# Convolution's ends reordered, norm and projection in one block; the last block's sixteen row copies issued by three engines

## Chip, core and metric

One core of a Trainium2 chip runs the kernel. Its engines are TensorE (PE in the profile, its weight loads PEld), VectorE (DVE), ScalarE (ACT), GpSimd (POOL) and SyncE (SP), which only issues transfers. ACT and POOL can issue transfers too. The metric is the device time of one execution in microseconds (us), as the median of several.

## What is computed

One step of a two-layer decoder trunk for 512 prompt tokens and 8 x 4 sample tokens (544 in all), 1024 channels, float32. Layer 0 mixes by sliding-window attention, layer 1 by a convolution module; each is followed by a mixture of 32 experts. The change is in the convolution module:

```python
def conv_module(h, hist, w_pw1, b_pw1, w_dw, b_dw, ln_g, ln_b, w_pw2, b_pw2):
    a = jnp.einsum('btd,de->bte', h, w_pw1) + b_pw1
    u = a[..., :D_CONV] * jax.nn.sigmoid(a[..., D_CONV:])
    ext = jnp.concatenate([hist.astype(u.dtype), u], axis=1)
    c = lax.conv_general_dilated(ext, w_dw[:, None, :].astype(ext.dtype), ...) + b_dw   # 31 taps, each channel by itself
    c = jax.nn.silu(layer_norm(c, ln_g, ln_b))
    y = jnp.einsum('btc,cd->btd', c, w_pw2) + b_pw2
    return y, ext[:, -(CONV_WIDTH - 1):]
```

Its input h is rmsnorm(x); x = x + y follows, then the experts on rmsnorm(x).

## The kernel before

Activations lie with channels on the 128 partitions: eight slices (KT = 8) of 128 channels by 544 tokens, a row of 544 being two halves of 272 (TH). A product in nearly full precision is made of float32r halves: a weight or operand is split into a high part (ACT, `high` and `x_high`) and a low part (DVE, or GpSimd for some, `low` and `x_low`), and TensorE adds high x high, high x low and low x high. So 128 output columns are 8 slices x 3 products x 2 halves of the tokens = 48 matmuls. The class `Columns` holds this: two weight buffers s, the semaphores `ready` (split), `projected` (multiplied), `x_ready`.

Each engine has its own list of instructions, in the order in which its function writes them, and waits on semaphores; there is no planner. A `nc.Block()` ends when all engines are through; `semaphores_back()` clears semaphores between stages, with a barrier of all engines.

`conv_stage` works in eight blocks of 128 channels. TensorE's order is written out: `value_columns(0)`, `gate_columns(0)`, the sums of squares for the rms norm (`square_sums`), the turning of the tap weights (`turn_taps`), and then for k = 1 to 7 values(k), gates(k), taps(k-1), sums(k-2), and at the end sums(6), taps(7), sums(7). The 31 taps of a block are shared: twenty on TensorE, by matmuls over `u_quads`, a copy of the block's rows in four shifts, and eleven on DVE, a chain of instructions each waiting for the one before. The copy is sixteen transfers of 32 partitions from SBUF to SBUF, eight issued by SP and eight by ACT (`load_quads`). DVE's `finish(k)` adds TensorE's taps to its own; `sums(k)` is the column sum for the layer norm's mean. GpSimd adds the squares in pairs, spreads tap weights (`weigh`) and does the taps of the sample tokens (`samples`). Before block 0, DVE's `x_low` instructions, the four copies of the convolution's history and a memset stand mixed in one list, and ACT's `x_high` and `square` alternate.

`layernorm_stage` is a block of its own: DVE subtracts the mean (eight instructions), ACT squares, TensorE sums the squares with a matrix of ones (128 output columns, so that every partition gets the sum), ACT takes the root over 128 x 544. TensorE also turns rows that DVE then copies out and SP stores. After it comes `semaphores_back()`, and then `project_back_stage`: a reciprocal over 128 x 544, then slice by slice scaling (DVE), silu and `x_high` (ACT), `x_low` (DVE or GpSimd), first all of column block 0, then all of column block 1, then six more, each added to x by DVE (`add`). SP loads router weights, the later columns, and then the first three experts' weights; the expert stage follows.

## Time and profile before

| | us |
|---|---|
| median of 3 runs | 1113.31 |
| lowest, highest | 1110.83, 1115.28 |
| the profiled execution, its own time | 1110.85 |
| its span from first to last instruction | 1108.8 |
| TensorE busy, mean granted clock | 929.0 (84%), 0.921 |

The span is what the trace covers; what lies around it is 2.05 us in this execution. All times below are us from the span's start in that one execution. The convolution stage lies at 533 to 710, the layer norm at 710 to 721, the projection at 722 to 790. A busy time in one stretch is summed over an engine's instructions, and overlapping matmuls are counted once.

### The profile page before, as it was taken

What the parts mean: (1) busy time and instruction counts of PE and PEld (TensorE: products, weight loads), DVE (VectorE), ACT (ScalarE), POOL (GpSimd) and SP (SyncE); (2) the same over time, 40 slices, a digit from 0 to 9 for tenths busy, and PEclk for the clock granted to TensorE, in tenths of its full rate; (3) what the DMA queues carried; (4) which work ended last, traced back from release to release, by engine and by line L of the source; (5) the groups of instructions that cost most, each with busy time, mean ns of one, the idle gap of its engine ahead of it and who ended that gap; (6) DMA issues with size and microseconds to landing.
All of it is one profiled execution on the core that took longest, in us unless ns stands there. A gap on an engine that the chain in (4) does not pass through costs nothing. (4 is left out here: it accounts for less than half of the span.)

```text
span 1108.8 us, 18939 instructions
## 1 busy us (share of the span) xinstructions
PE 929.0 (84%) x7248; PEld 674.9 (61%) x7248; DVE 421.2 (38%) x948; ACT 286.1 (26%) x591; POOL 271.3 (24%) x423
## 2 busy tenths in 40 slices
PE   6999988967997788884679999669869988788757
PEld 5878878954554455553677877359645545454535
DVE  5167763263111111113768786573551111111115
ACT  6356561132111111111521111262312111111103
POOL 0800000014432322221234353120033432322120
PEclk8999999978999998997789999889969998898998
DMA  7521112695999999965534452325859999999925
GB/s 232 162 52 39 39 40 59 247 397 208 418 417 417 418 417 417 420 274 187 135 79 119 116 144 56 79 65 219 363 216 388 415 417 418 418 419 419 390 81 200
DMA packets 111690, 277.55 MB, mean 250 GB/s; under 512 B 35404, under 2 KB 73628, under 8 KB 86986
## 3 DMA queue, kind: packets, MB, share of 16 engines
q1 hardware_dynamic: 96054, 253.74, 60.0%
q0 software_dynamic: 11424, 17.87, 4.4%
q10 hardware_dynamic: 4132, 4.86, 1.8%
q8 instruction: 51, 0.84, 0.3%
q14 instruction: 29, 0.24, 0.1%
HBM read 266.25 MB, written 27.45 MB: 265 GB/s over the span
## 5 line engine op out<-in xcount | busy, mean ns | idle before, releaser
L1763 PE MATMUL ps<-ring,areaB 128*64 128x256 f32 x672 | 170.7, 412 | 38.3 <-issue 22.4
L1797 DVE COPY areaB<-ps 128x512 f32<-128x512 f32 x66 | 45.6, 691 | 378.3 <-PE ps L1780 378.3
L1764 PE MATMUL ps<-ring,areaB 128*64 128x256 f32 x672 | 171.1, 413 | 0.0
L1763 PEld LDWEIGHTS ps<-ring,areaB 128*64 128x64 f32 x672 | 96.2, 148 | 90.0 <-issue 30.8
L1809 POOL DMA_INDIRECT pair_rows<-areaB,idx x66 | 67.8, 1027 | 276.6 <-DVE areaB L1797 257.9
L1788 ACT ACTIVATE v_rows<-ps 128x256 f32<-128x256 f32 x66 | 25.3, 383 | 294.0 <-PE ps L1764 294.0
L1022 PE MATMUL ps<-conv_x_high,pw_halves 128*128 128x272 f32 x512 | 91.3, 298 | 9.6 <-DVE conv_x_low L1302 5.4
L1764 PEld LDWEIGHTS ps<-ring,areaB 128*64 128x64 f32 x672 | 96.1, 148 | 0.0
L1022 PEld LDWEIGHTS ps<-conv_x_high,pw_halves 128*128 128x128 f32 x512 | 76.0, 195 | 12.1 <-DVE conv_x_low L1302 5.3
L1804 POOL DMA_INDIRECT areaC<-h_rows,idx x66 | 68.6, 1039 | 55.8 <-issue 44.5
L1780 PE MATMUL ps<-ring,areaB 128*64 128x512 f32 x336 | 79.9, 593 | 1.4 <-DVE areaB L1794 1.4
L1785 ACT ACTIVATE areaB<-ps 128x512 f32<-128x512 f32 x66 | 39.4, 597 | 149.6 <-PE ps L1755 149.6
L1755 PEld LDWEIGHTS ps<-ident,areaC 128*128 128x128 f32 x264 | 28.8, 145 | 64.0 <-issue 48.7
L451 PE MATMUL ps<-mix_x_high,w_halves_A 128*128 128x272 f32 x320 | 59.7, 298 | 6.2 <-DVE w_halves_A L814 6.2
L1763 PE MATMUL ps<-areaA,areaB 128*64 128x256 f32 x192 | 48.6, 411 | 12.9 <-issue 10.5
L1763 PE MATMUL ps<-h_T,areaB 128*64 128x256 f32 x192 | 48.8, 413 | 12.3 <-issue 10.8
L1755 PE MATMUL ps<-ident,areaC 128*128 128x128 f32 x264 | 45.1, 295 | 14.2 <-DMA areaC<-h_rows,idx 14.2
L1022 PE MATMUL ps<-x_high,w_halves_C 128*128 128x272 f32 x256 | 47.3, 300 | 11.1 <-POOL x_low L1000 10.3
L1347 DVE SCALAR_TENSOR_TENSOR ps<-areaB,chan,ps 128x512 f32<-128x512 f32 x72 | 54.4, 756 | 2.6
L629 PE MATMUL ps<-o_high,w_halves_A 128*128 128x272 f32 x256 | 52.1, 297 | 3.7 <-DVE o_low L947 2.2
L1563 POOL IOTA areaS<- 128x10 f32 x2 | 0.3, 157 | 223.1 <-POOLq L113 171.6
L1022 PE MATMUL ps<-conv_x_low,pw_halves 128*128 128x272 f32 x256 | 54.3, 294 | 0.0
(348 smaller groups left out, 1806.7 us busy)
## 6 DMA issues: line engine op xcount, KB each, us to landing
ring<-in_w_gate SPq DMA_DIRECT2D x40, 1024.0 KB, 22.8
ring<-in_w_up SPq DMA_DIRECT2D x40, 1024.0 KB, 28.2
ring<-in_w_down SPq DMA_DIRECT2D x40, 1024.0 KB, 27.9
areaA<-in_w_gate SPq DMA_DIRECT2D x12, 1024.0 KB, 23.1
areaA<-in_w_up SPq DMA_DIRECT2D x12, 1024.0 KB, 28.7
wring<-in_w_down SPq DMA_DIRECT2D x12, 1024.0 KB, 28.1
h_T<-in_w_gate SPq DMA_DIRECT2D x12, 1024.0 KB, 23.6
h_T<-in_w_up SPq DMA_DIRECT2D x12, 1024.0 KB, 29.6
```

The costliest lines, as they stand in the source:

```text
L451: mm = pe.matmul(ps[:, bank + c, 0:TH], w[:, s, which, k, :], x[:, k, c * TH:(c + 1) * TH], start=(k == 0 and which == 0 and x is x_high), ...
L629: mm = pe.matmul(ps[:, 2 + n % 2 + 2 * c, 0:TH], w[:, s, which, k, :], o[:, k, c * TH:(c + 1) * TH], start=(k == 0 and which == 0 and o is ...
L1022: mm = pe.matmul(ps[:, 2 * s + c, 0:TH], self.w[:, s, w, k, :], self.x[x][:, k, c * TH:(c + 1) * TH], start=(k == 0 and w == 0 and x == 0) ...
L1347: steps.link(v.scalar_tensor_tensor(vec_acc if j < CW - 1 else c_T[:, k, 0:NP], shifted(k, j), col(k, V_DW + j), vec_acc, ALU.mult, ALU.add))
L1755: mm = pe.transpose(ps[:, odd, j * P:(j + 1) * P], rows_in[:, s, j * P:(j + 1) * P], ident[:, :])
L1763: pe.matmul(ps[0:CAP, 2 + odd, 0:F], rows, ring_gate(ws)[:, k, :], start=(k == 0), stop=(k == KT - 1))
L1764: mm = pe.matmul(ps[CAP:P, 2 + odd, 0:F], rows, ring_up(ws)[:, k, :], start=(k == 0), stop=(k == KT - 1))
L1780: mm = pe.matmul(ps[c * CAP:(c + 1) * CAP, 5 + odd, :], hid_T[:, s, k, :], ring_down(ws)[:, k, c * HALF:(c + 1) * HALF], start=(k == 0), s ...
L1785: return nc.scalar.activation(rows_T[:, s].rearrange("p j r -> p (j r)"), ps[:, odd, :], ACT.Copy)
L1797: return v.tensor_copy(rows_out[:, s, :], ps[:, 5 + odd, :])
L1804: return gp.indirect_dma_start(rows_in[:, s, :], None, h_half_rows, bass.IndirectOffsetOnAxis(idx[:, s:s + 1], 0), bounds_check=2 * T - 1, ...
L1809: return gp.indirect_dma_start(pair_half_rows, bass.IndirectOffsetOnAxis(idx[:, RING + s:RING + 1 + s], 0), rows_out[:, s, :], None, bound ...
```

## The change

- **Head of `conv_stage`.** ACT makes all eight `x_high` first, then splits the gate weights, then squares; then it splits the value weights of block 1, ahead of the root. DVE makes all eight `x_low` first, then the gate weights' low half, then copies the history, then the low half of block 1's value weights, ahead of the reciprocal; in block 0 it scales the values before the gates. SP loads block 1's weights before it waits for the history.
- **Tail of `conv_stage`.** DVE runs `finish(6)` before its own taps of block 7. Block 7's sixteen copies are issued six by SP, six by ACT, four by GpSimd, which has them ahead of its `samples(7)` and signals on a semaphore of its own; TensorE's taps wait for both. SP issues the first `w_pw2` columns here.
- **Norm and projection** are one block, `layernorm_project_stage`; `semaphores_back()` stands before it. ACT splits both first columns' high halves before the squares. The sums of squares use 64 output columns for each half of the tokens, side by side on the partitions; root and reciprocal work on 128 x 272, and two matmuls spread the result over the partitions into PSUM, where DVE's scaling reads it. DVE makes both low halves between the reciprocal and the scaling. TensorE does column blocks 0 and 1 together, slice by slice, after which the others follow as before. SP stores the turned rows before it loads the later columns.

The diff, cut (what is left out in the new function are lines that stood in the two old ones):

```diff
-            def x_lows(self, v, source, scale=None):
...
             def multiply(self, pe, s, n, first=False):
                 pe.wait_ge(self.ready[s], n + 1)
                 for k in range(KT):
                     if first:
                         pe.wait_ge(self.x_ready[k % 2], k // 2 + 1)
-                    for w, x in ((0, 0), (0, 1), (1, 0)):
-                        for c in range(2):
-                            mm = pe.matmul(ps[:, 2 * s + c, 0:TH], self.w[:, s, w, k, :], self.x[x][:, k, c * TH:(c + 1) * TH],
-                                           start=(k == 0 and w == 0 and x == 0), stop=(k == KT - 1 and w == 1))
+                    mm = self.multiply_part(pe, s, k)
                 mm.then_inc(self.projected[s], 1)
+            def multiply_part(self, pe, s, k):
+                for w, x in ((0, 0), (0, 1), (1, 0)):
+                    for c in range(2):
+                        mm = pe.matmul(ps[:, 2 * s + c, 0:TH], self.w[:, s, w, k, :], self.x[x][:, k, c * TH:(c + 1) * TH],
+                                       start=(k == 0 and w == 0 and x == 0), stop=(k == KT - 1 and w == 1))
+                return mm
...
-        def project_back_stage(name, w, w_halves, operand, norm, offset, l, rows_stored, stores):
...
+                quarter = lambda i: [(i, g) for g in range(4)]
+                def load_quads(eng, k, copies, landed=None):
                     eng.wait_ge(u_done, 2 * k + 2)
                     after(eng, taps_done, k - 1)
-                    for i in shifts:
-                        for g in range(4):
-                            eng.dma_start(u_quads[32 * i:32 * i + 32, k % 2, g, :],
-                                          u_T[32 * g:32 * g + 32, k, i:i + UQ]).then_inc(quads_landed[k % 2], 16)
+                    for i, g in copies:
+                        eng.dma_start(u_quads[32 * i:32 * i + 32, k % 2, g, :],
+                                      u_T[32 * g:32 * g + 32, k, i:i + UQ]).then_inc(landed or quads_landed[k % 2], 16)
                 @block.sync
                 def _(sp):
...
-                    sp.wait_ge(hist_ready, 1)
                     for k in range(KT):
                         for i in range(2):
                             if k + 1 < KT:
                                 sp.wait_ge(cols.ready[i], k + 1)
                                 sp.dma_start(wring[:, i], columns(w, (k + 1) * P + i * D)).then_inc(cols.landed[i], 16)
-                        load_quads(sp, k, (0, 1))
+                        if k == 0:
+                            sp.wait_ge(hist_ready, 1)
+                        load_quads(sp, k, quarter(0) + quarter(1)[0:4 if k + 1 < KT else 2])
+                    for i in range(2):
+                        sp.wait_ge(cols.ready[i], KT)
+                    first_columns(sp, "w_pw2", w_pw2[0], (0, P))
                     sp.wait_ge(stored, 16)
...
                     def taps(k):
                         pe.wait_ge(tap_weights_ready, k + 1)
-                        pe.wait_ge(quads_landed[k % 2], 16 * 16 * (k // 2 + 1))
+                        pe.wait_ge(quads_landed[k % 2], 16 * 16 * (k // 2 + 1) - (64 if k == KT - 1 else 0))
+                        if k == KT - 1:
+                            pe.wait_ge(last_quarter_landed, 64)
...
                     cols.high(act, 0, 0)
                     for k in range(KT):
                         x_high(k)
+                    cols.high(act, 1, 0)
+                    for k in range(KT):
                         square(k)
-                    cols.high(act, 1, 0)
+                    cols.high(act, 0, 1)
                     act.wait_ge(summed, 1)
                     nc.scalar.activation(half(std), sum_banks, ACT.Sqrt, scale=1.0 / D, bias=eps_col).then_inc(rooted, 1)
                     act.wait_ge(tap_cols_turned, 1)
                     nc.scalar.activation(tap_cols_flat, pe_acc[:, 0:KT * 4 * QUADS], ACT.Copy).then_inc(tap_cols_kept, 1)
                     for k in range(KT):
-                        if k + 1 < KT:
+                        if 0 < k < KT - 1:
                             cols.high(act, 0, k + 1)
                         sigmoid(k)
                         if k + 1 < KT:
                             cols.high(act, 1, k + 1)
-                        load_quads(act, k, (2, 3))
+                        load_quads(act, k, quarter(2) + (quarter(3) if k + 1 < KT else quarter(1)[2:4]))
...
                     cols.low(v, 0, 0)
-                    v.wait_ge(state_turned, 1)
                     for k in range(KT):
                         x_low(k)
-                        if 1 <= k <= 4:
-                            copy_history((k - 1) // 2, (k - 1) % 2)
-                        if k == 5:
-                            v.wait_ge(hist_copied, 4)
-                            v.memset(u_T[:, :, 0:HIST], 0.0).then_inc(hist_ready, 1)
                     cols.low(v, 1, 0)
+                    v.wait_ge(state_turned, 1)
+                    for i in range(2):
+                        for c in range(2):
+                            copy_history(i, c)
+                    v.wait_ge(hist_copied, 4)
+                    v.memset(u_T[:, :, 0:HIST], 0.0).then_inc(hist_ready, 1)
+                    cols.low(v, 0, 1)
                     v.wait_ge(rooted, 1)
                     v.reciprocal(rstd, std).then_inc(inverted, 1)
                     v.wait_ge(inverted, 1)
-                    def scale(k):
+                    def scale_gate(k):
...
+                    def scale_value(k):
...
                     for k in range(KT):
-                        if k + 1 < KT:
+                        if 0 < k < KT - 1:
                             cols.low(v, 0, k + 1)
-                        scale(k)
+                        if k == 0:
+                            scale_value(k)
+                        scale_gate(k)
+                        if k > 0:
+                            scale_value(k)
                         glu(k)
                         if k + 1 < KT:
                             cols.low(v, 1, k + 1)
+                        if k == KT - 1:
+                            finish(k - 1)
                         taps(k)
-                        if k >= 1:
+                        if 0 < k < KT - 1:
                             finish(k - 1)
                     finish(KT - 1)
...
                     for k in range(KT):
                         if k + 1 < KT:
                             weigh(k + 1)
+                        else:
+                            load_quads(gp, k, quarter(3), last_quarter_landed)
                         samples(k)
...
-        def layernorm_stage():
+        def layernorm_project_stage(l):
...
+            ln_sq = areaS[:, 2048:2048 + 2 * T].rearrange("p (b t) -> p b t", b=2)
+            rstd_rows = ln_std[:, 0:TH]
+            rstd_wide = ps[:, 4:6, 0:TH]
...
             with nc.Block() as block:
+                @block.sync
+                def _(sp):
...
+                    sp.wait_ge(u_kept, 2)
+                    sp.dma_start(conv_prompt[0, 0], tail).then_inc(u_stored, 16)
+                    for b in range(NB):
+                        sp.dma_start(conv_sample[0, b, HIST - NQ:HIST, :], fresh[NQ * b:NQ * b + NQ, :]).then_inc(u_stored, 16)
+                    with sp.Fori(1, 4) as n:
+                        for s in range(2):
+                            sp.wait_ge(cols.ready[s], n)
+                            sp.dma_start(wring[:, s], columns(w_pw2[0], (2 * n + s) * P)).then_inc(cols.landed[s], 16)
+                    for s in range(3):
+                        load_gateup(sp, l, s, s)
+                        load_down(sp, l, s, s)
+                    sp.wait_ge(u_stored, 16 * (1 + NB))
+                @block.gpsimd
+                def _(gp):
+                    for k in range(0, KT, 2):
+                        cols.x_low(gp, c_T, k)
                 @block.tensor
                 def _(pe):
...
                     for k in range(KT):
+                        pe.wait_ge(ln_squared, k + 1)
+                        for c in range(2):
+                            mm = pe.matmul(ps[64 * c:64 * c + 64, 4, 0:TH], ones[:, 0:64], ln_sq[:, k % 2, c * TH:(c + 1) * TH],
+                                           start=(k == 0), stop=(k == KT - 1))
+                        mm.then_inc(ln_summed, 1)
+                    pe.wait_ge(inverted, 1)
+                    for c in range(2):
+                        mm = pe.matmul(rstd_wide[:, c, :], ones[64 * c:64 * c + 1, :], rstd_rows[64 * c:64 * c + 1, :], start=True, stop=True)
+                    mm.then_inc(spread, 1)
...
+                    pe.wait_ge(u_kept, 2)
+                    for s in range(2):
+                        pe.wait_ge(cols.ready[s], 1)
+                    for k in range(KT):
+                        pe.wait_ge(cols.x_ready[k % 2], k // 2 + 1)
+                        for s in range(2):
+                            mm = cols.multiply_part(pe, s, k)
+                            if k == KT - 1:
+                                mm.then_inc(cols.projected[s], 1)
...
                 @block.vector
                 def _(v):
...
+                    v.wait_ge(rooted, 1)
+                    v.reciprocal(rstd_rows, rstd_rows).then_inc(inverted, 1)
+                    for s in range(2):
+                        cols.low(v, s, 0)
+                    v.wait_ge(spread, 1)
+                    v.wait_ge(centred, KT)
+                    for k in range(KT + 2):
+                        if k < KT:
+                            v.tensor_tensor(half(c_T[:, k, :]), half(c_T[:, k, :]), rstd_wide, ALU.mult).then_inc(scaled, 1)
+                        if k >= 3 and k % 2:
+                            cols.x_low(v, c_T, k - 2)
...
                 @block.scalar
                 def _(act):
+                    for s in range(2):
+                        cols.high(act, s, 0)
                     for k in range(KT):
                         act.wait_ge(centred, k + 1)
                         if k >= 2:
+                            act.wait_ge(ln_summed, k - 1)
+                        nc.scalar.activation(ln_sq[:, k % 2, :], c_T[:, k, :], ACT.Square).then_inc(ln_squared, 1)
+                    act.wait_ge(ln_summed, KT)
+                    nc.scalar.activation(rstd_rows, ps[:, 4, 0:TH], ACT.Sqrt, scale=1.0 / D, bias=eps_col).then_inc(rooted, 1)
+                    for k in range(KT):
+                        act.wait_ge(scaled, k + 1)
+                        nc.scalar.activation(c_T[:, k, :], c_T[:, k, :], ACT.Silu,
+                                             scale=chan[:, k, V_LNG:V_LNG + 1], bias=chan[:, k, V_LNB:V_LNB + 1]).then_inc(out, 1)
+                        act.wait_ge(out, k + 1)
+                        cols.x_high(c_T, k)
...
-        layernorm_stage()
         semaphores_back()
-        project_back_stage("w_pw2", w_pw2[0], w_halves_C, c_T, True, V_BPW2, 1, u_stored, 1 + NB)
+        layernorm_project_stage(1)
```

## Rows read from the trace of the kernel before

**Rows 1.** Busy us by stretch: PE, PEld, DVE, ACT, POOL, granted clock, transfers.

```profile
569.50:574.20 4.70, 4.67 (x21) 4.67 (x22) 4.36 (x7) 1.08 (x2) 3.47 (x4) 0.51 0.41 99
574.20:583.80 9.60, 9.60 (x78) 9.47 (x76) 7.25 (x9) 1.06 (x1) 3.42 (x7) 1.00 0.68 175
569.50:688.40 118.90, 118.86 (x932) 97.70 (x932) 92.20 (x122) 17.61 (x20) 49.84 (x76) 0.98 0.46 118
...
729.40:734.40 5.00, 4.76 (x18) 4.16 (x19) 5.00 (x7) 4.38 (x7) 1.49 (x2) 0.50 0.34 104
```

**Rows 2.** Instructions of three lines, head: ns min/median/max, first to last start.

```profile
L1271 ACT ACTIVATE conv_x_high<-x_T,chan x8: 731/734/738, 535.3 to 543.6; 128x544 fp32r<-128x544 f32 x8
...
L1302 DVE SCALAR_TENSOR_TENSOR conv_x_low<-x_T,chan,conv_x_high x8: 656/1054/1882, 536.7 to 547.6; 128x544 fp32r<-128x544 f32 x8
...
L1370 POOL TENSOR_TENSOR h_T<-h_T x4: 1344/1352/1599, 537.8 to 545.0; 128x544 f32<-128x544 f32 x4
```

**Rows 3.** Timeline, 556 to 571: start, us, engine, line, [idle before, releaser].

```profile
556.78 3.83 PE L1221 MATMUL ps<-h_T,ones 128*128 128x272 f32 x16
...
561.39 3.55 DVE L1322 RECIPROCAL areaS<-areaS 128x544 f32<-128x544 f32 x1 [11.84 <-ACT areaS L1287]
...
564.96 0.40 PE L1231 MATMUL ps<-ident,ring 31*32 31x5 f32 x17 [2.27 <-issue]
...
568.77 0.71 DVE L1331 TENSOR_TENSOR areaS<-ps,areaS 128x544 f32<-128x544 f32 x1
...
569.53 0.82 PE L1022 MATMUL ps<-conv_x_high,pw_halves 128*128 128x272 f32 x2 [4.18 <-DVE areaS L1331]
...
570.61 1.23 DVE L993 TENSOR_TENSOR pw_halves<-wring,pw_halves 128x1024 fp32r<-128x1024 f32 x1
```

**Rows 4.** Transfers issued from 569 to 710: KB each, median us to landing.

```profile
wring<-in_w_pw SPq DMA_DIRECT2D x13, 512.0 KB, 5.4
ring<-areaB SPq DMA_DIRECT2D x64, 66.0 KB, 2.1
```

**Rows 5.** Timeline, tail of the convolution, 688 to 710.

```profile
688.43 4.50 PE L1241 MATMUL ps<-ring,areaS 128*32 128x512 f32 x40
...
691.09 4.97 SPq L1183 DMA_DIRECT2D ring<-areaB  x8
691.09 5.32 ACTq L1183 DMA_DIRECT2D ring<-areaB  x8
...
691.95 7.09 DVE L1347 SCALAR_TENSOR_TENSOR ps<-areaB,chan,ps 128x512 f32<-128x512 f32 x9
...
697.21 0.24 POOL L1395 TENSOR_TENSOR areaA<-areaA,chan 128x32 f32<-128x32 f32 x1
...
699.85 0.69 DVE L1352 TENSOR_TENSOR areaA<-ps,areaA 128x512 f32<-128x512 f32 x1
...
702.71 5.01 PE L1241 MATMUL ps<-ring,areaS 128*32 128x512 f32 x40
...
708.55 1.19 PE L1249 MATMUL ps<-areaA,ones 128*128 128x272 f32 x4 [0.82 <-DVE areaA L1352]
```

**Rows 6.** Instructions of one line: GpSimd's indirect transfers in the expert stages.

```profile
L1809 POOL DMA_INDIRECT pair_rows<-areaB,idx x66: 981/1032/1042, 271.4 to 1073.7; - x66
```

**Rows 7.** Timeline, norm and projection, 710 to 754.

```profile
710.03 0.29 DVE L1433 COPY areaS<-areaB 128x256 f32<-128x256 f32 x1 [1.53 <-PEq L1177]
...
720.18 0.71 ACT L1457 ACTIVATE areaS<-ps,small 128x544 f32<-128x544 f32 x1
...
722.00 1.06 ACT L989 ACTIVATE w_halves_C<-wring 128x1024 fp32r<-128x1024 f32 x1 [1.10 <-PEq L113]
...
729.46 0.79 PE L1022 MATMUL ps<-x_high,w_halves_C 128*128 128x272 f32 x2 [9.35 <-POOL x_low L1000]
...
753.06 0.71 PE L1066 MATMUL ps<-areaB,ones 128*64 128x256 f32 x4
```

**Rows 8.** Instructions of one line: the projection's silu on ACT.

```profile
L1121 ACT ACTIVATE areaA<-areaA,chan x8: 825/827/841, 726.4 to 737.1; 128x544 f32<-128x544 f32 x8
```

More of the change, by code:

```diff
@@ L1001, in x_low @@
                                   ALU.subtract).then_inc(self.x_ready[k % 2], 1)
-            def x_lows(self, v, source, scale=None):
-                for k in range(KT + 2):
-                    if scale and k < KT:
-                        scale(k)
-                    if k == 1:
-                        self.low(v, 0, 0)
-                    if k >= 3 and k % 2:
-                        self.x_low(v, source, k - 2)
-                self.low(v, 1, 0)
             def multiply(self, pe, s, n, first=False):
@@ L1425, in _, with sums @@
+                    mm.then_inc(spread, 1)
+                    def sums(k, s, first, last):
                         pe.wait_ge(squared, k + 1)
                         for c in range(2):
-                            mm = pe.matmul(ps[:, 2 + c, 0:TH], ones[:, :], sq[:, k % 2, c * TH:(c + 1) * TH],
-                                           start=(k == 0), stop=(k == KT - 1))
+                            mm = pe.matmul(ps[64 * c:64 * c + 64, 6, 0:(256, T - 256)[c]], ones[:, 0:64], sq[:, s, (0, 256)[c]:(256, T)[c]],
+                                           start=first, stop=last)
@@ L1431, in _, with turn @@
+                    def turn(n):
+                        for s in range(2):
+                            pe.wait_ge(added[s], n)
+                            cols.multiply(pe, s, n)
+                            sums(2 * n + s - 2, s, isinstance(n, int) and n == 1 and s == 0, False)
+                    turn(1)
+                    with pe.Fori(2, 4) as n:
+                        turn(n)
+                    for s in range(2):
+                        sums(KT - 2 + s, s, False, s == 1)
                 @block.vector
@@ new lines, in add @@
+                    def add(n, last):
+                        for s in range(2):
+                            v.wait_ge(cols.projected[s], n + 1)
+                            xs = half(x_T[:, ds(2 * n + s, 1), :].rearrange("p k t -> p (k t)"))
+                            off = chan[:, ds(2 * n + s, 1), V_BPW2:V_BPW2 + 1].rearrange("p k n -> p (k n)")
+                            v.scalar_tensor_tensor(xs, ps[:, 2 * s:2 * s + 2, 0:TH], off, xs,
+                                                   ALU.add, ALU.add).then_inc(added[s], 1)
+                            if not last:
+                                cols.low(v, s, n + 1)
@@ L1449, in _ @@
+                    with v.Fori(0, 3) as n:
+                        add(n, False)
+                    v.wait_ge(route_landed[l], 64)
+                    v.tensor_tensor(w_route[:, :, :], w_route[:, :, :], chan[:, :, V_FFN + l:V_FFN + l + 1].to_broadcast([P, KT, NR]),
+                                    ALU.mult).then_inc(route_scaled[l], 1)
+                    add(3, True)
                 @block.scalar
                 def _(act):
+                    for s in range(2):
+                        cols.high(act, s, 0)
@@ L1453, in _, with square @@
                         if k >= 2:
-                            act.wait_ge(summed, k - 1)
-                        nc.scalar.activation(sq[:, k % 2, :], c_T[:, k, :], ACT.Square).then_inc(squared, 1)
-                    act.wait_ge(summed, KT)
-                    nc.scalar.activation(half(ln_std), ps[:, 2:4, 0:TH], ACT.Sqrt, scale=1.0 / D, bias=eps_col).then_inc(rooted, 1)
-                    act.wait_ge(rooted, 1)
+                            act.wait_ge(ln_summed, k - 1)
[8 more added lines that the diff above has]
+                        cols.x_high(c_T, k)
+                    def square(n, first, last):
+                        for s in range(2):
+                            if not last:
+                                cols.high(act, s, n + 1)
+                            act.wait_ge(added[s], n + 1)
+                            if not first:
+                                act.wait_ge(summed, 2 * n + s - 1)
+                            nc.scalar.activation(sq[:, s, :], x_T[:, ds(2 * n + s, 1), :].rearrange("p k t -> p (k t)"),
+                                                 ACT.Square).then_inc(squared, 1)
+                    square(0, True, False)
+                    with act.Fori(1, 3) as n:
+                        square(n, False, False)
+                    square(3, False, True)
         area_route = areaS[:, :]
```

134 lines of the change are left out of this document (20 added, 114 removed).

## The prediction

> **What bounds the kernel now.** I read the busy time by stage first. From 569.5 to 688.4 TensorE has 118.86 us of work in 118.9 us [rows 1]: seven of the convolution's eight blocks run at its pace, and nothing the change does to other engines there can show. So I looked for TensorE's idle time at the ends of the stage, in the timeline, and found three places where it waits for a chain of other engines.
>
> The first is the head. The value and gate columns of block 0 should be 96 matmuls of 0.125 us (9.60 us for 76 to 78 of them at the full clock [rows 1]), 12.1 us, but they run from 537.7 to 556.8: DVE's split of the input (the x_low instructions) feeds them, at 0.66 us each alone and 1.88 beside GpSimd's additions, with history copies in between [rows 2]. Then comes a chain: square sums, root, reciprocal, the split of the next weights, gate scaling, value scaling, and TensorE starts block 1 at 569.53 after 4.18 us idle [rows 3].
>
> The second is the tail. DVE's own taps of block 7 run from 691.10 to 699.82; only then does it finish block 6 (699.85), for which TensorE's sums wait, and behind those the taps of block 7, at 702.71 [rows 5]. Their copies had landed long before: 2.1 us after issues that end at 696.4 [rows 4, 5].
>
> The third is the layer norm and the start of the projection: TensorE's first projection matmul comes at 729.46, and its clock stays at 0.50, the 1.2 GHz level, to 734.4 [rows 1, 7].
>
> Behind all this the expert stage waits for the projection. Its first loads are issued when the last projection columns are split, so they come earlier with it. I know of nothing later that would hold still, so a gain here should reach the end whole.
>
> **The change, part by part.** I keep the clock of the profiled execution.
>
> *Head.* ACT's eight x_high instructions now come without squares between them: 535.3 + 8 x 0.73 = 541.1 at the latest; the gate columns' high half (1.05) to 542.2. DVE's x_lows have no copies and no additions beside them: the last ends at about 542.0, the gate's low half (1.23 [rows 3]) at 543.4. TensorE: values 537.7 + 6.05 = 543.7, gates to 549.8. Meanwhile ACT squares (1.19 a pair before [rows 2], so some 0.5 each without the x_high, an estimate) to 546.2; GpSimd adds from 543.2, four times 1.35, to 548.6. The copies and the memset took what the x_lows left of 536.7 to 548.4, about 11.7 - 8 x 1.05 = 3.3 us, so the history is ready at 546.7. All three are done before 549.8, and cost nothing; if GpSimd took 1.6 for each (its longest [rows 2]) it would still be 549.6. The value weights of block 1, whose split moves ahead of the root, are loaded earlier because SP no longer waits for the history first: issued at about 537, landed 5.4 us later [rows 4], high half after the squares (547.3), low half at 548.5.
>
> Then sums 3.83 [rows 3] to 553.6, root 0.71 (the same shape in rows 7) to 554.4, reciprocal 3.55 [rows 3] to 558.0, and value scaling, now first, 0.71 to 558.7. The tap turning on TensorE ends 4.75 us after the sums, with the same 2.27 us pause, at 558.4. Block 1 starts at 558.7 instead of 569.53: **10.8 us**. From 569.5 to 574.2 the granted clock was 0.51: 21 matmuls took 4.7 us instead of 2.65 [rows 1]. I leave that loss in. With the shorter wait it may go, worth up to 2.05, of which the DVE chain behind the first sigmoid lets 1.6 through (12.4 in all). The other bound: TensorE at half speed for 3 us in the first pass, with some contention between DVE and GpSimd: 8.
>
> *Middle.* Blocks 1 to 6 keep their order, so their pace stays.
>
> *Tail.* The taps of block 6 end at 688.43 + 4.50 = 692.93, so block 6 is finished at 693.65. DVE's own taps, 8.76 us from 691.09 to the next instruction [rows 5], now end at 702.4. The last finish (0.69) ends at 703.1 and the last sums (1.19) at 704.35, against 709.74 before: **5.4 us**. This needs TensorE's taps done by 702.4, so begun by 697.9 (4.50 at the full clock) or 697.4 (5.01). SP's six copies are issued by 691.1 + 6 x 0.62 = 694.8, ACT's by 695.1; the last start 0.65 before that and land 2.1 later, by 696.6. A plain copy from GpSimd is not in the trace. From below its cost is SP's 0.62; the nearest row on GpSimd is the indirect transfer, 0.98 to 1.04 [rows 6]. I take 1.03: the fourth starts at 694.2 and lands at about 696.6. Behind the four copies in GpSimd's queue stand the samples of block 7, 6.3 us: now 695.2 to 701.5 instead of 697.45, and only the last sums (703.1) wait for them. So the copies are free up to (703.1 - 6.3 - 691.1) / 4 = 1.4 us each; above that each 0.1 costs 0.4.
>
> A rule speaks against this part. The rows first: each of DVE's ten instructions here writes or reads PSUM, and GpSimd's 66 indirect transfers keep within 0.98 to 1.04 us [rows 5, 6] in stages where DVE works too. The Trainium skill (SBUF — State Buffer, section "SBUF: two separate sides") says that a transfer issued by GpSimd cannot get its descriptors written while DVE runs an instruction that takes both shared ports, so it seems blocked until DVE is done. The page names a copy from SBUF to SBUF as such an instruction; by the rows none is in this chain. By the rule at its widest the copies would land after DVE's chain; that is a rival below.
>
> *Norm and projection.* The semaphore clearing moves to the front: 1.10 us at that boundary [rows 7] instead of 0.3 (709.74 to 710.03) there, so the block starts 0.8 later after the last sums; the boundary behind the norm goes. Counted from the block's first instruction: two weight high halves first, 2.1; then squares. The new sums use half the output columns, two beside each other; the nearest row is 0.71 for four [rows 7]. With two buffers, two squares take 0.66 + 0.71 + some 0.13 of handing over, 0.75 each: the last square ends at 7.9, the table load (1.28) at 9.2, the half-width root at 9.6, the half-width reciprocal (1.8) at 11.4. The two low halves stand between it and the scaling: 2.35, to 13.8, covering the spreading matmuls. The first silu comes at 14.55; before, 726.4 - 710.03 = 16.4 [rows 7, 8].
>
> TensorE started 3.06 us after the first silu; so now at 17.6. It then does both columns by slices, 96 matmuls. Operand pace is 10.7 / 7 = 1.53 us a slice [rows 8], the matmuls 1.5, so nothing starves. At half speed for 4.8 us, as before (some 21 matmuls), and 75 x 0.126 after: 31.9. Before, both columns were done at 747.4, 37.4 after the block's start, and the next followed at once. Now both end together, so the next column waits for its high (1.06) and low half (1.23) from 31.1 on: 33.5. So 3.9 gained, less 0.8: **3.1 us**. All fast: 5.3. At half speed for another 5 us: 0.5.
>
> Sum: 10.8 + 5.4 + 3.1 = 19.3. The profiled execution took 1110.85 (span 1108.8 and 2.05 around it), which gives 1091.6. The median of the three runs, 1113.31, lies 2.5 higher, so the median after may too; I stay by the sum and say 1092.
>
> **Rivals.**
> (a) The clock helps: TensorE stays fast into block 1 and sooner into the projection. 12.4 + 5.4 + 5 = 22.8, 1088. For it: the shorter waits. Against: the 2.27 us pause in the tap turning stays. 18%.
> (b) The head gives less: 8 or below, because DVE and GpSimd slow each other (0.66 against 1.88 in rows 2) or the clock falls in the first pass. With 3 to 6 lost, 1095 to 1098. 17%.
> (c) GpSimd's copies come late: they land behind DVE's chain, 702.4 + 2.1, taps 5.0, finish and sums 1.9: 711.5, later than before by 1.8. The gain is 19.3 - 5.4 - 1.8 = 12.1: 1099. This is the page's rule as a mechanism here. 6%.
> (d) Slower: a plain GpSimd copy is dear. It holds back the samples and with them the last sums; above 1.4 us each, 4 us are lost for every further 1. The whole gain is gone at 6.2 us a copy, and 1117 is reached at 7.6. For it: the row is missing. Against: 1.03 for the nearest. 3%.
> (e) The gain does not arrive: some later wait that I overlooked takes it. 1108 to 1112. For it: the expert stage is dense with loads. Against: they are issued by the projection's own progress. 4%.
>
> **How the numbers follow.** The forecast has the other 52%, its own range is 1089 to 1095. The range 1086.5 to 1100 takes in (a), (b) and (c). A change of 0.5%, 5.6 us, is about what this measurement can tell from none. Faster: all but (d) and (e), 0.93; same 0.04; slower 0.03.
>
> **What would show it.** In the profile after: block 1's first matmul 21 us after block 0's first instead of 32; x_lows at 0.66 us; one stretch of full TensorE time of about 119 us unchanged; block 6 finished before DVE's last taps; last taps on TensorE starting some 5 us earlier relative to block 7's gates; GpSimd copies near 1 us; both projection columns done together, then a bubble of about 2 us. The prediction is wrong if the first pass still takes over 15 us, if a GpSimd copy takes over 1.4, or if the merged block starves TensorE.

## The result

The median fell from 1113.24 to 1094.26 us (four runs, 1093.52 to 1099.47): a ratio of 0.984, 95% interval 0.980 to 0.988. The prediction was 1092.0, within 1086.5 to 1100. The profiled execution took 1094.44 (span 1092.7), so the span is 16.1 us shorter.

I compare the two profiles stretch by stretch, each counted from its own first instruction. The head first. This is the timeline of the changed kernel (start, us, engine, line, what it does, idle time before and its releaser):

```profile
534.46 3.43 PE L1089 MATMUL ps<-ident,areaA 120*128 120x120 f32 x16 [1.93 <-PEq L113]
...
537.60 0.79 PE L1015 MATMUL ps<-conv_x_high,pw_halves 128*128 128x272 f32 x2
...
551.10 3.83 PE L1106 MATMUL ps<-h_T,ones 128*128 128x272 f32 x16
...
555.71 3.55 DVE L1212 RECIPROCAL areaS<-areaS 128x544 f32<-128x544 f32 x1 [5.75 <-ACT areaS L1176]
559.30 0.72 DVE L1223 TENSOR_TENSOR areaS<-ps,areaS 128x544 f32<-128x544 f32 x1
...
560.08 0.82 PE L1015 MATMUL ps<-conv_x_high,pw_halves 128*128 128x272 f32 x2 [0.26 <-DVE areaS L1223]
```

From the first transpose to block 1's first matmul it is 560.08 - 534.46 = 25.62 us. Before, block 1's first matmul came at 569.53 [rows 3] and the first transpose at 533.27:

```profile
533.27 3.42 PE L1204 MATMUL ps<-ident,areaA 120*128 120x120 f32 x16 [1.93 <-PEq L113]
```

That is 36.26, so 10.64 are gained. TensorE's idle time ahead of block 1 went from 4.18 to 0.26, and the first pass from 19.1 to 13.5 us. From block 1's first matmul to the taps of block 6 both kernels take the same time within 0.04 us.

The tail of the convolution, same view:

```profile
678.94 4.50 PE L1128 MATMUL ps<-ring,areaS 128*32 128x512 f32 x40
...
681.60 4.78 SPq L1064 DMA_DIRECT2D ring<-areaB  x6
681.60 4.79 ACTq L1064 DMA_DIRECT2D ring<-areaB  x6
681.88 2.12 POOL L1064 DMA_DIRECT2D ring<-areaB  x4 [8.29 <-DVE areaB L1230]
683.37 2.10 PE L1136 MATMUL ps<-areaA,ones 128*128 128x272 f32 x8
683.50 0.69 DVE L1244 TENSOR_TENSOR areaA<-ps,areaA 128x512 f32<-128x512 f32 x1 [1.93 <-PE ps L1128]
...
684.95 7.09 DVE L1239 SCALAR_TENSOR_TENSOR ps<-areaB,chan,ps 128x512 f32<-128x512 f32 x9
...
689.00 4.50 PE L1128 MATMUL ps<-ring,areaS 128*32 128x512 f32 x40 [3.53 <-DMA ring<-areaB]
692.08 0.75 DVE L1239 SCALAR_TENSOR_TENSOR areaA<-areaB,chan,ps 128x512 f32<-128x512 f32 x1
693.63 0.69 DVE L1244 TENSOR_TENSOR areaA<-ps,areaA 128x512 f32<-128x512 f32 x1 [0.80 <-PE ps L1128]
694.37 1.18 PE L1136 MATMUL ps<-areaA,ones 128*128 128x272 f32 x4 [0.87 <-DVE areaA L1244]
```

Block 6 is finished at 683.50, ahead of DVE's own taps, as the change orders it. But the last taps now wait for their copies: the releaser at 689.00 is the DMA, 7.40 us after the first issue. DVE's chain ends at 692.83 and the last finish still waits 0.80 for TensorE. From block 6's taps to the end of the last sums it is 16.61 us against 21.31 [rows 5]: 4.70 gained.

The copies by queue (ns min/median/max of one issue, first and last start):

```profile
L1064 SPq DMA_DIRECT2D ring<-areaB x6: 508/666/1184, 681.6 to 685.2; - x6
L1064 ACTq DMA_DIRECT2D ring<-areaB x6: 517/739/1154, 681.6 to 685.7; - x6
L1064 POOL DMA_DIRECT2D ring<-areaB x4: 498/516/607, 681.9 to 683.5; - x4
...
DMA to landing us min/median/max: 2.0/3.3/3.8
```

GpSimd's copy is the cheapest of the three, and the time to landing rose from 2.1 [rows 4] to 3.3.

Norm and projection, timeline of the changed kernel:

```profile
696.48 0.29 DVE L1398 COPY areaS<-areaB 128x256 f32<-128x256 f32 x1 [2.16 <-PEq L113]
...
705.37 0.49 ACT L1445 ACTIVATE areaS<-ps,small 128x272 f32<-128x272 f32 x1
...
707.66 2.29 DVE L993 TENSOR_TENSOR w_halves_C<-wring,w_halves_C 128x1024 fp32r<-128x1024 f32 x2
707.80 1.19 PE L1364 MATMUL ps<-areaS,ones 1*128 1x272 f32 x4 [3.01 <-DVE areaS L1406]
...
709.87 2.61 DVE L1414 TENSOR_TENSOR areaA<-areaA,ps 128x544 f32<-128x544 f32 x4
710.62 0.84 ACT L1448 ACTIVATE areaA<-areaA,chan 128x544 f32<-128x544 f32 x1 [3.46 <-DVE areaA L1414]
...
713.70 0.79 PE L1015 MATMUL ps<-x_high,w_halves_C 128*128 128x272 f32 x2 [4.72 <-POOL x_low L1000]
...
729.79 0.49 PE L1015 MATMUL ps<-x_high,w_halves_C 128*128 128x272 f32 x2 [1.81 <-DVE w_halves_C L993]
...
773.08 5.85 DVE L1652 TENSOR_SCALAR h_T<-x_T,chan 128x544 f32<-128x544 f32 x8 [1.95 <-PEq L1324]
```

The same two places of the kernel before, where the third column follows the second without a pause:

```profile
746.97 0.41 PE L1022 MATMUL ps<-x_high,w_halves_C 128*128 128x272 f32 x2
...
790.04 5.84 DVE L1644 TENSOR_SCALAR h_T<-x_T,chan 128x544 f32<-128x544 f32 x8 [1.78 <-PEq L1040]
```

From the block's start to the third column's first matmul it is 33.31 us against 746.97 - 710.03 = 36.94: 3.63 gained. The boundary ahead of the block costs 0.93 instead of 0.29. From the end of the convolution's last sums to the route stage's first scaling of h_T by DVE it is 77.53 against 790.04 - 709.74 = 80.30: 2.8 in all.

The sum: 10.6 + 4.7 + 2.8 = 18.1 us since the convolution began. Against that, the changed kernel's span is 1.2 longer ahead of the convolution and 0.9 longer behind the projection.

### The profile page after: what moved, and what is told of

Its sections match the earlier page's. It is cut to its first block and busy times, and to the rows that moved or that the text cites. A ratio compares the mean times of both kernels' runs of the same rounds, so it can differ in the third digit from the quotient of the medians.

```text
span 1092.7 us, 18939 instructions
## 1 busy us (share of the span) xinstructions
PE 920.3 (84%) x7252; PEld 669.2 (61%) x7252; DVE 412.7 (38%) x948; ACT 285.4 (26%) x591; POOL 273.3 (25%) x427
## 5 line engine op out<-in xcount | busy, mean ns | idle before, releaser
L1771 PE MATMUL ps<-ring,areaB 128*64 128x256 f32 x672 | 169.0, 409 | 39.3 <-issue 23.3
L1772 PE MATMUL ps<-ring,areaB 128*64 128x256 f32 x672 | 169.3, 409 | 0.0
L1771 PE MATMUL ps<-areaA,areaB 128*64 128x256 f32 x192 | 45.5, 392 | 12.1 <-issue 10.2
L451 PEld LDWEIGHTS ps<-mix_x_high,w_halves_A 128*128 128x128 f32 x320 | 47.9, 193 | 8.8 <-issue 8.8
```

Of the source, the lines that this page charges most:

```text
L451: mm = pe.matmul(ps[:, bank + c, 0:TH], w[:, s, which, k, :], x[:, k, c * TH:(c + 1) * TH], start=(k == 0 and which == 0 and x is x_high), ...
L1771: pe.matmul(ps[0:CAP, 2 + odd, 0:F], rows, ring_gate(ws)[:, k, :], start=(k == 0), stop=(k == KT - 1))
L1772: mm = pe.matmul(ps[CAP:P, 2 + odd, 0:F], rows, ring_up(ws)[:, k, :], start=(k == 0), stop=(k == KT - 1))
```

## The experiments

I read two figures in every profile: **copies to taps** (first copy issue of block 7 to TensorE's last taps) and the **tail** (block 6's taps to the end of the last sums; 16.61 after, 21.31 before). For norm and projection it is the 77.53 us above. In the diffs, minus is the changed kernel (for x3, the kernel before), and ... stands for lines left out.

### x1: the third queue taken away

```
-load_quads(sp, k, quarter(0) + quarter(1)[0:4 if k + 1 < KT else 2])
+load_quads(sp, k, quarter(0) + quarter(1))
...
-load_quads(act, k, quarter(2) + (quarter(3) if k + 1 < KT else quarter(1)[2:4]))
+load_quads(act, k, quarter(2) + quarter(3))
...
-load_quads(gp, k, quarter(3), last_quarter_landed)
```

> The changed kernel with block 7's sixteen copies issued eight by SP and eight by ACT again. In the changed kernel TensorE's last taps begin 7.4 us after the first of these copies is issued, and the last ones wait for a transfer. Theory (the copies go at the rate of the transfers, three queues only share it): 7.0 to 7.7, conv's end moves by less than 0.4. Rival (the queues' issue time sets it: eight at 0.80 instead of six): about 9, and the convolution ends 1.5 later.

One run, 1091.65 us. Copies to taps is 7.00 (679.49 to 686.49), less than the 7.40 with three queues; the tail is 16.22:

```profile
679.49 4.95 SPq L1064 DMA_DIRECT2D ring<-areaB  x8
679.49 5.30 ACTq L1064 DMA_DIRECT2D ring<-areaB  x8
...
686.49 4.50 PE L1126 MATMUL ps<-ring,areaS 128*32 128x512 f32 x40 [3.14 <-issue]
```

The third queue gained nothing and cost some 0.4 us: copies to taps is 6.96 to 7.05 in the three profiles with two queues (x1, x3, x8) and 7.32 to 7.53 in the seven with three queues and whole rows. The copies of x1 by queue:

```profile
L1064 SPq DMA_DIRECT2D ring<-areaB x8: 508/591/598, 679.5 to 683.8; - x8
L1064 ACTq DMA_DIRECT2D ring<-areaB x8: 518/612/873, 679.5 to 684.2; - x8
...
DMA to landing us min/median/max: 2.0/2.1/2.4
```

Two queues are not held up: their issues take 0.6 us and land 2.1 later, and the last of eight such issues plus one landing is already 7.0. So the theory's figure came out, but with two queues the pace of the issues explains it as well as that of the transfers. With three queues the issues stretch to 0.80 and the landing to 3.3.

### x2: the projection's first columns loaded after the copies

```
+sp.wait_ge(quads_landed[1], 16 * 16 * (KT // 2) - 64)
+sp.wait_ge(last_quarter_landed, 64)
 first_columns(sp, "w_pw2", w_pw2[0], (0, P))
```

> The changed kernel with the first w_pw2 columns loaded only after block 7's copies have landed. Theory (the 1 MB of weights that SP issues behind its copies slows the last of them: landing 3.3 us instead of 2.1): the last taps begin 6.2 to 6.6 us after the first copy's issue instead of 7.4, and the last finish follows DVE's chain, so that the stage ends 0.8 earlier. Rival (the sixteen copies fill the transfer engines by themselves): still 7.2 to 7.6, no gain.

One run, 1097.58. Copies to taps is 7.32: the two weight loads behind them are not what delays the copies. The tail is 18.23, because the last taps took 6.20 us instead of 4.50. This was new, and is taken up under x9.

### xa: half the bytes

```
+n = UQ if k + 1 < KT else UQ // 2
-eng.dma_start(u_quads[32 * i:32 * i + 32, k % 2, g, :], u_T[32 * g:32 * g + 32, k, i:i + UQ])
+eng.dma_start(u_quads[32 * i:32 * i + 32, k % 2, g, 0:n], u_T[32 * g:32 * g + 32, k, i:i + n])
```

> The changed kernel whose sixteen copies for the last block carry only the first half of each row (the other half of the ring keeps what an earlier block left, so the convolution's last block is not computed in full): the same 16 issues on the same three queues with half the bytes. Theory (the copies fill the transfer engines: DMA share 0.86 to 0.91 while they run): last taps begin 5.0 to 6.0 us after the first issue (7.40 in the changed kernel), issues of SP and ACT back to about 0.6 us each; the stretch from the sixth block's taps to the last sums is then bounded by VectorE's own taps at 15.5 to 16.0 us. Rival (packets, queues or the issuing set it): 6.8 us or more.

The second half of each row is not copied, so block 7 is not computed in full, and only the convolution of this run is read: it took 7219 us in all, since its values send the routing another way, with 322 of GpSimd's indirect transfers in the expert stages instead of 66.

```profile
678.25 3.69 SPq L1065 DMA_DIRECT2D ring<-areaB  x6
678.25 4.02 ACTq L1065 DMA_DIRECT2D ring<-areaB  x6
678.53 2.12 POOL L1065 DMA_DIRECT2D ring<-areaB  x4 [8.29 <-DVE areaB L1231]
...
683.65 4.50 PE L1129 MATMUL ps<-ring,areaS 128*32 128x512 f32 x40 [1.53 <-DMA ring<-areaB]
...
690.26 1.18 PE L1137 MATMUL ps<-areaA,ones 128*128 128x272 f32 x4 [2.11 <-DVE areaA L1245]
```

Copies to taps is 5.40 and the tail 691.44 - 675.59 = 15.85, now bounded by DVE. With as many issues on the same queues, half the bytes land 2.0 us earlier, SP's issues are back at 0.62 us from 0.80, and the median landing is back at 2.1: with three queues it is the bytes that hold up issues and landing. The prediction's 5.5 would have needed half of them; the transfers cost the tail 16.61 - 15.85 = 0.76 us.

### x3: of the tail's change, only the order of the finish

The kernel before, with `finish(6)` ahead of DVE's taps of block 7.

```
+if k == KT - 1:
+    finish(k - 1)
 taps(k)
-if k >= 1:
+if 0 < k < KT - 1:
     finish(k - 1)
```

> The kernel before with one change: block 6 is finished ahead of DVE's own taps of block 7. Theory (the order on DVE is the tail's whole gain): from the first taps matmul of block 6 to the end of the last sums 16.4 to 17.0 us instead of 21.3, the time 4.3 to 4.9 below before (ratio 0.996). Rival (the copies by a third queue are needed): 18 us or more, the time at most 3 below.

1109.53 against 1113.43 us, ratio 0.9968 (0.9948 to 0.9988). In its profile copies to taps is 6.96 with two queues, and the tail is 19.11. Taken by itself that is the rival's side (18 or more), but its last taps took 7.42 us; the granted clock was 0.50 up to 704.0 and 0.70 after:

```profile
693.35 5.32 ACTq L1183 DMA_DIRECT2D ring<-areaB  x8
...
700.31 7.42 PE L1241 MATMUL ps<-ring,areaS 128*32 128x512 f32 x40 [3.10 <-issue]
```

At 4.50 us they would end 2.9 earlier and the tail would be 16.2, that of x1. By this estimate the one edit is the tail's whole gain. The medians differ by 3.9 us, the interval reaches from 1.3 to 5.8: more than nothing, and open between theory and rival.

### x4: the early weight split and the order of scaling undone

Block 1's value weights are split behind the root again, and in block 0 the gate is scaled ahead of the value.

```
-cols.high(act, 0, 1)
...
-cols.low(v, 0, 1)
 v.wait_ge(rooted, 1)
...
-if k == 0:
-    scale_value(k)
 scale_gate(k)
...
+scale_value(k)
```

> The changed kernel with the split of block 1's value weights back between root and scaling, and gates scaled before values in block 0. From the stage's first transpose to block 1's first matmul: 36.3 us before, 25.6 in the changed kernel. Theory (3.2 of the gain is the split, 0.65 the order of scaling, the rest the unmixed input split): 29.2 to 29.8. Rival (the first pass gives nearly all, the split hides behind the tap turning): 25.6 to 27.

One run, 1101.16. First transpose to block 1 is 28.14 us. Its first pass ran at the full clock; in the changed kernel's executions where that was so (x0 below) the stretch is 24.24. At equal clock these edits together are worth 3.9 us, the 3.2 + 0.65 of the theory, though 28.14 itself lies under its 29.2. What is left of the head's change, above all the unmixed split of the input, is then 36.26 - 28.14 = 8.1, at the clocks of these two profiles. The tail is 19.5, with last taps of 7.45.

### x5: norm and projection in two blocks again

> The changed kernel with the old norm and projection put back as two blocks (rows kept and added to inside the norm's block, one first column, the projection's weights fetched where they were before). Theory (the one block saves 2.8 us between the end of the convolution's last sums and the route stage's first scaling of h_T by VectorE: 80.3 us before, 77.5 us after): that stretch returns to 79.8 to 80.8 us, and head and tail of the convolution stay as after (25.6 and 16.6 us, the tail up to 3 us longer if the last taps run at the lower clock). Rival (part of the 2.8 us comes from elsewhere, such as the clock of the projection or the transfers that the convolution leaves behind): the stretch stays under 79 us.

One run, 1098.91. From the end of the last sums (696.21) to h_T:

```profile
776.54 5.85 DVE L1666 TENSOR_SCALAR h_T<-x_T,chan 128x544 f32<-128x544 f32 x8 [1.78 <-PEq L1044]
```

This is 80.33 us, the 80.30 of before (80.32 in x3, which has the old blocks too): the 2.8 are the one block's. With the changed blocks the stretch is 77.4 to 78.1 in x1, x2, x4, xa and xb, and 79.53 in x0.

### x6: slices in another order

```
-for k in range(KT):
-    for s in range(2):
+order = [(k, s) for k in range(4) for s in range(2)] + [(k, s) for s in range(2) for k in range(4, KT)]
+for k, s in order:
```

> The changed kernel with the first two projection columns multiplied in another order: slices 0 to 3 of both in turn, then slices 4 to 7 of the first, then those of the second, so that the first column is complete four slices earlier. Theory (the 1.81 us bubble of TensorE ahead of the third column's first matmul is the chain high half, sum, low half that begins only when the first column is complete): bubble 0 to 0.4 us, third column's first matmul 31.5 to 31.9 us after the block's start (33.3 in the changed kernel), the rest of the projection unchanged. Rival (the low half's VectorE work is held by something else, such as the second column's sum): bubble 1.4 to 1.9 us, 33 us or more.

One run, 1090.83. TensorE's rows from 712.75 to 733.35 show no idle time, the bubble of 1.81 is gone, and the stretch to h_T is 770.50 - 694.60 = 75.90: 1.63 gained. The cause was the chain behind the first column.

### x7: the first low half ahead of the root

```
+cols.low(v, 0, 0)
 v.wait_ge(rooted, 1)
...
-for s in range(2):
-    cols.low(v, s, 0)
+cols.low(v, 1, 0)
```

> The changed kernel with the low half of the first projection column computed by VectorE ahead of its wait for the root, where it stands idle, and not between the reciprocal and the scalings. Theory (two low halves of 2.29 us end 0.9 us later than the spread of the inverse over the partitions by TensorE): first scaling 0.8 to 1.0 us earlier, first silu 13.1 to 13.4 us after the block's start (14.14 in the changed kernel), third column's first matmul 0.8 to 1.0 us earlier than 33.31. Rival (the silus wait for ScalarE's table or the spread): 0.3 us or less.

One run, 1095.11. From the root to the first scaling it is 711.02 - 707.66 = 3.36 us, against 4.50: 1.14 gained there. The first silu came 14.24 after the block's start, not 13.1 to 13.4, since the root itself was 1.24 later: TensorE's transposes took 0.42 us each instead of 0.27, at a granted clock of 0.51 from 698.2 to 701.1 (1.00 in the changed kernel's first profile). So the stretch to h_T shows only 0.1 of it, and the total is inconclusive.

### x0, x8, x9, xb: the changed kernel again, a better one, and the clock of the last taps

x8 has the edits of x1, x6 and x7. x9 is x8, and xb is x1, with

```
 sums(KT - 2)
+pe.wait_ge(u_done, 2 * KT)
+for n in range(24):
+    pe.matmul(ps[:, 0, 0:TH], cols.w[:, 0, 0, 0, :], cols.x[0][:, 0, 0:TH], start=True, stop=True)
 taps(KT - 1)
```

> The changed kernel itself, timed again beside the next three on one chip. Expected: 1093 to 1099 us, 14 to 19 us under the kernel before; last taps of the convolution between 4.5 us (TensorE granted its full clock) and 7.4 us (half) in the profiled execution.

> The changed kernel with three edits: the last block's copies back on SP and ACT, eight each; the first two projection columns in the order of slices that closed the bubble; the first low half ahead of the wait for the root. Theory (the three lie one after another on the path that sets the end: 0.4, 1.6 and 1.1 to 1.4 us): convolution's end to the route stage's first scaling of h_T 74.4 to 75.0 us (77.5), median 2.5 to 3.5 us under the changed kernel. Rival (the earlier silus meet x_low on VectorE and GpSimd, or the lower clock of the last taps hides it): under 1.5 us.

> The kernel of the three edits, with 24 more matmuls of TensorE (128 by 272, their result not used) between the sums of the seventh block and the last taps, where it else stands idle for 3.1 to 3.6 us. Theory (that idle stretch is why the last taps run at half the clock in most profiles: 7.42, 7.45, 6.20, 6.20, 5.80 us against 4.50 in two): last taps 4.5 us in the profile and the median 1 to 2.5 us under the same kernel without them. Rival (the clock falls whatever TensorE does there, and the added matmuls hold the taps up): last taps over 5.5 us or later than 7.5 us after the first copy, and no gain.

> The changed kernel with the last block's copies on SP and ACT, and the 24 added matmuls ahead of the last taps, without the two edits of norm and projection. Theory: last taps 4.5 us, median 1.4 to 3 us under the changed kernel (0.4 for the copies, the rest for the clock). Rival (added matmuls cost what they give): within 1 us of the changed kernel.

Five or six runs each on one chip, the kernel before at 1112.61:

| kernel | median (range), us | ratio to before (95%) | idle before last taps | last taps | copies to taps | tail | to h_T |
|---|---|---|---|---|---|---|---|
| x0, changed kernel | 1097.08 (1095.23 to 1098.99) | 0.986 (0.983 to 0.988) | 3.55 | 5.79 | 7.42 | 17.92 | 79.53 |
| x8, three edits | 1092.36 (1089.96 to 1093.06) | 0.981 (0.978 to 0.983) | 3.19 | 4.50 | 7.05 | 16.26 | 74.83 |
| x9, x8 filled | 1093.17 (1089.65 to 1098.65) | 0.983 (0.980 to 0.986) | 1.51 | 4.50 | 8.42 | 17.63 | 74.86 |
| xb, x1 filled | 1095.68 (1093.05 to 1101.93) | 0.986 (0.984 to 0.989) | 0.77 | 4.50 | 7.67 | 16.89 | 77.60 |

x0 is 15.5 us under the kernel before. x8 has the lowest median, 4.7 us under x0, more than the 2.5 to 3.5 expected; its stretch to h_T came out as forecast (74.4 to 75.0), 2.7 under the 77.53 of the first profile. In x0's profile the stretch is another 2.0 longer: TensorE's transposes there took 0.42 us each, as in x7, and the granted clock from 716 to 724 was 0.64. By how much such stretches part the two medians is not known.

The granted clock (column PEclk, before the last two) around the last taps: in x0, in x8 ahead of them, and in x9:

```profile
685.00:688.40 3.40, 0.00 (x0) 0.03 (x1) 3.22 (x6) 0.00 (x0) 3.17 (x5) 0.89 0.84 224
688.40:692.00 3.60, 3.59 (x24) 1.13 (x28) 3.46 (x5) 0.00 (x0) 1.03 (x4) 0.63 0.80 223
```

```profile
685.00:688.00 3.00, 0.00 (x0) 0.00 (x0) 2.86 (x5) 0.00 (x0) 2.05 (x5) 1.00 0.83 208
```

```profile
684.00:687.80 3.80, 3.46 (x26) 3.17 (x24) 3.66 (x5) 0.00 (x0) 2.53 (x6) 1.00 0.56 132
...
684.00:685.00 1.00, 1.00 (x8) 0.93 (x7) 0.96 (x2) 0.00 (x0) 0.92 (x2) 1.00 0.95 226
...
686.00:687.00 1.00, 1.00 (x10) 1.00 (x9) 0.96 (x2) 0.00 (x0) 0.77 (x3) 1.00 0.07 13
```

With the added matmuls the clock stayed at its 2.4 GHz level, but the copies landed 0.7 (xb) to 1.4 us (x9) later than with the same queues and no added matmuls. They were not slowed evenly: in x9 they moved 226 GB/s beside the first microsecond of added matmuls (x8, with none, had 208), and then next to nothing from 685.6 to 687.0, with one SP issue of 2.16 us; in xb they all but stopped from 684.8 to 685.5. The Trainium skill (SBUF — State Buffer, section "SBUF: two separate sides") says that a transfer cannot be slowed by computing; that first microsecond agrees, and what stopped the copies for 1.4 and 0.7 us is not settled.

x9 lies 0.8 over x8, with late copies and no gain, as its rival said. xb lies 1.4 under x0, the least that its theory allowed, 0.4 of it for the two queues; the intervals overlap, so it decides nothing. For the clock, both have last taps of 4.50, as x8 has without the added matmuls, so the theory is not refuted and not shown.

## Why the prediction was right, and where its terms were off

**Head (10.8; measured 10.64).** The size is right through two errors that cancel. The first pass began 3.14 us after the first transpose, not 4.4: I had kept the old start. In the kernel before, DVE's first x_low also waits for the last of the transposes, and the columns wait for it; the change put that wait behind the x_lows, which my list of steps left out. In the profile before, the first weights came as late as the transposes (split from 534.33 on). In x3, which has the old order, the weights were split from 535.15 on, at once, and still the pass began 5.56 us after the first transpose:

```profile
535.17 3.43 PE L1204 MATMUL ps<-ident,areaA 120*128 120x120 f32 x16 [1.93 <-PEq L113]
...
538.64 2.64 DVE L1302 SCALAR_TENSOR_TENSOR conv_x_low<-x_T,chan,conv_x_high 128x544 fp32r<-128x544 f32 x2 [1.18 <-PE ps L1204]
...
540.73 0.49 PE L1022 MATMUL ps<-conv_x_high,pw_halves 128*128 128x272 f32 x2 [2.12 <-DVE conv_x_low L1302]
```

The second error: I ran the pass at the full clock (12.1 us), while here its first part was at the 1.2 GHz level and it took 13.5. Windows of the changed kernel, then of x0, where it was not:

```profile
537.00:540.00 3.00, 3.00 (x15) 2.95 (x14) 3.00 (x5) 3.00 (x6) 0.00 (x0) 0.50 0.47 176
540.00:543.00 3.00, 3.00 (x23) 3.00 (x23) 3.00 (x5) 3.00 (x5) 0.26 (x1) 0.89 0.54 163
```

```profile
537.00:540.00 3.00, 3.00 (x24) 2.90 (x23) 3.00 (x5) 3.00 (x5) 0.00 (x0) 0.92 0.48 176
```

x0's head is 558.83 - 534.59 = 24.24, a gain of 12.0. Of the eleven profiles with the whole change of the head, seven gave 24.2 to 24.5 and four 25.2 to 25.6. One more term was off and hidden: block 1's value weights were split from 547.64 on, after a wait for their transfer, though I had them landed at 542.4; TensorE was still at block 0. Of rival (b) the clock half came, worth 1.4 and not 3. Rival (a) did not come at either place: from 560.1 to 564.0 the granted clock was 0.50, from 713.7 to 718.0 again 0.50.

**Tail (5.4; measured 4.70).** The step that failed is "the last start 0.65 before that and land 2.1 later": it took issue and landing times from blocks in which copies were issued at the pace of two queues, and added the issues of a third. In place of 0.62 us an issue of SP took 0.80, so that the last copy was issued 4.1 us after the first and not 3.4, and the landing took 3.3 and not 2.1. Sixteen copies of 66 KB need 7.0 us by two queues and 7.3 to 7.5 by three, with or without the loads behind them (x1, x2), and 5.4 with half the bytes (xa). The Trainium skill (Trainium Kernel Development and Optimization, section "Key Constraints") says that transfers of all three issuers share the same engines and that more issuers save issue time alone; the runs agree, and I had not weighed it. So TensorE's taps began after the limit that I had set for them. The condition's second half was also too mild: it allowed 5.01 us for the taps, and they took 4.50 to 7.45. With the changed kernel's three queues the tail was 16.61 us in the first profile, 17.92 to 18.24 in x0, x2, x5, x6 and x7, and 19.50 in x4: a gain of 1.8 to 4.7.

**GpSimd's copies (1.03 each; measured 0.53).** They took less than the 0.62 that I had set as the cost from below. Rivals (c) and (d) are out: the copies did not wait for DVE's chain, and GpSimd's samples, from 684.01 to 690.32, delayed no sums. That leaves the Trainium skill's rule behind (c) almost untested: at 0.53 us each, three of the four issues fell into DVE's idle time from 681.57 to 683.50, and the fourth, beside the finish, took no more than 0.61.

**Norm and projection (3.1; measured 2.8).** The new block's parts held: third column at 33.31 for 33.5, the boundary 0.64 and not 0.8, first silu 14.14 after the start for 14.55, bubble 1.81 for 2. What was off is the old end: I read 37.4 where the trace has 36.94, so the block could give 3.4 by my own terms and gave 3.63. The last 0.2 were lost in the columns that follow. x5 shows the whole, x6 the bubble.

**Arrival at the end (rival e).** It arrived but for 0.9 us behind the projection, which is within what executions differ by there: from the first scaling of h_T to the end it is 318.8 us before and 320.5 in x3, whose code there is the same, 319.6 after and 320.1 in x0. The medians fell by 19.0 and, on the other chip, 15.5 us (x0), around the 18.1 of the stretches; the prediction's sum was 19.3. Part of the miss is the base: 1092.0 is that sum taken from the fastest execution before; from the median of 1113.24 it would have given 1093.9, against 1094.26.

## What to carry to other kernels

When copies that follow each other are spread over more queues, ask first whether the transfer engines have room: time the landing of the last one from the first issue, not of one copy alone. Where TensorE must wait, price the work behind the wait at both levels of its clock. And where two results end together and the next step needs only one, let that one end early: an order of loops gave back 1.6 us.

## What the hardware showed

I had not expected the clock to decide so much. After 3.1 to 3.7 us without work TensorE's last 40 tap matmuls took 4.50 us in three profiles and 5.79 to 7.45 in seven, with the same program giving either (4.50 in the first profile of the changed kernel, 5.79 in x0); after 1.5 us or less they took 4.50 in all three. These three are few, and the fill's cost hides what it is worth. A plain copy issued by GpSimd took it 0.52 us (median), under SP's 0.59 and ACT's 0.61 in x1.
